# Order of the first products of the second block, and where the first tile's expert sums live, in a two-block transformer kernel on one core

## What is computed

```python
# first block, for each tile of 128 tokens
u = jnp.take(expert_u, eidx, axis=0)                      # 8 heads x 16 rows a token
h = jax.nn.gelu(jnp.einsum('thkd,td->thk', u, xb))
vv = jnp.take(expert_v, eidx, axis=0)
x = x + jnp.einsum('thk,thkd->td', (g * h), vv)
# second block
n = rmsnorm(x, norm_mix_pre);  proj = n @ w_in            # pool input, q, k, v, xq, gates
mem_n = rmsnorm(mem, norm_mem);  kv = mem_n @ w_mem_kv
# then stick-breaking attention, pooling, memory attention, gates, and a feed-forward
```

## Time and profile before

| what | value |
|---|---|
| three runs | 1216.73, 1220.64, 1221.88 us |
| profiled execution, its own time | 1221.03 us |
| its span in the trace | 1218.3 us, mean granted TensorE clock 0.981 |
| TensorE matmul busy | 1074.5 us (88%) |
| VectorE busy | 807.4 us (66%) |
| ScalarE busy | 387.3 us (32%) |
| GpSimd busy | 271.9 us (22%) |
| DMA | 372.42 MB, 306 GB/s over the span |

### The profile page before, as it was taken

The page is one execution under the profiler, slowest core; times in us unless marked ns, Lnnn a source line. Parts: engine busy times, 40 slices in busy tenths (PEclk is TensorE's granted clock), DMA queues, the critical chain, the costliest instruction groups (busy, mean ns, idle before and its releaser), DMA issues.

```text
span 1218.3 us, 12645 instructions
## 1 busy us (share of the span) xinstructions
PE 1074.5 (88%) x4502; PEld 701.4 (58%) x4502; DVE 807.4 (66%) x1681; ACT 387.3 (32%) x705; POOL 271.9 (22%) x261
## 2 busy tenths in 40 slices
PE   6988499889998886898877777789999999999997
PEld 5877355435543342444322222268877778999986
DVE  4666687877777677877787776554655476555543
ACT  5654221122112111310121011035765435444432
POOL 0000244454344343433433433300000000000000
PEclk8999799999999999899999999989999999999999
DMA  9734599999999999899999999985433434555440
GB/s 362 272 139 183 213 418 419 420 420 419 418 419 420 420 421 419 330 419 420 420 420 419 420 419 421 420 324 185 150 135 141 173 142 153 176 191 187 173 173 35
DMA packets 54381, 372.42 MB, mean 306 GB/s; under 512 B 6064, under 2 KB 7216, under 8 KB 10544
## 3 DMA queue, kind: packets, MB, share of 16 engines
q0 software_dynamic: 36864, 268.45, 53.2%
q1 hardware_dynamic: 17456, 103.17, 23.0%
HBM read 370.55 MB, written 1.05 MB: 305 GB/s over the span
## 4 chain that ended last, share of the span: by engine, by line
PE 59%; DMA 28%; DVE 8%; issue 3%; ACT 1%; POOL 1%; SPq 0%; DVEq 0%; POOLq 0%; ACTq 0%
DMA uv<-in_peer_uv,eidx 28%; PE bank L1787 15%; PE bank L1559 11%; PE bank L1560 11%; PE bank L1561 11%; PE bank L1622 5%; DVE uv L1301 3%; DMA wraw<-in_in1a 1%; DVE diag L1315 1%; DVE w_lo L1064 1%; PE bank L1531 1%; POOL uv L604 1%; ACT w_hi L676 1%; PE bank L1770 1%; PE bank L1720 1%
## 5 line engine op out<-in xcount | busy, mean ns | idle before, releaser
L1787 PE MATMUL bank<-uv,diag 128*128 128x512 f32 x1024 | 492.1, 610 | 102.8 <-DVE diag L1315 101.4
L1301 DVE SCALAR_TENSOR_TENSOR uv<-uv,xn 128x1024 f32<-128x1024 f32 x256 | 313.9, 1226 | 155.3 <-DMA uv<-in_peer_uv,eidx 153.3
L1787 PEld LDWEIGHTS bank<-uv,diag 128*128 128x128 f32 x1024 | 181.0, 191 | 377.7 <-issue 375.9
L604 POOL DMA_INDIRECT uv<-in_peer_uv,eidx x256 | 271.5, 1061 | 514.2 <-PE bank L1787 368.2
L1064 DVE TENSOR_TENSOR w_lo<-wraw,w_hi 128x2048 fp32r<-128x2048 f32 x76 | 173.7, 2291 | 138.1 <-ACT w_hi L676 138.1
L853 ACT ACTIVATE chosen<-chosen 128x1 f32<-128x1 f32 x256 | 51.9, 203 | 506.1 <-DVE uv L1301 506.0
L676 ACT CAST w_hi<-wraw 128x2048 fp32r<-128x2048 f32 x76 | 144.5, 1905 | 91.0 <-PE bank L1561 81.4
L1559 PE MATMUL bank<-nT_hi,w_hi 128*128 128x256 f32 x432 | 123.8, 287 | 3.2 <-DVE nT_lo L1076 3.2
L1560 PE MATMUL bank<-nT_lo,w_hi 128*128 128x256 f32 x432 | 123.4, 286 | 0.0
L1561 PE MATMUL bank<-nT_hi,w_lo 128*128 128x256 f32 x432 | 123.4, 286 | 0.0
L1315 DVE TENSOR_SCALAR diag<-const,chosen 128x128 f32<-128x128 f32 x256 | 88.3, 345 | 0.3 <-ACT chosen L853 0.3
(11 more groups left out here) (245 smaller groups left out, 1151.4 us busy)
## 6 DMA issues: line engine op xcount, KB each, us to landing
wraw<-in_ff_in SPq DMA_DIRECT2D x22, 1024.0 KB, 4.7
wraw<-in_ff_out SPq DMA_DIRECT2D x11, 1024.0 KB, 4.8
wraw<-in_query SPq DMA_DIRECT2D x4, 1024.0 KB, 8.9
uv<-in_peer_uv,eidx POOLq DMA_INDIRECT x256, 13.5
apart_last<-in_query SPq DMA_DIRECT2D x4, 512.0 KB, 11.0
wraw<-in_in_q SPq DMA_DIRECT2D x2, 1024.0 KB, 6.0
wraw<-in_in_k SPq DMA_DIRECT2D x2, 1024.0 KB, 10.1
wraw<-in_pool_o SPq DMA_DIRECT2D x2, 1024.0 KB, 4.7
```

What stands on the lines that cost most here:

```text
L604: pool.indirect_dma_start(out=uv[:, n % RING, :], out_offset=None, in_=io["peer_uv"], in_offset=bass.IndirectOffsetOnAxis(ap=eidx[:, head ...
L1301: nc.vector.scalar_tensor_tensor(out=u, in0=u, scalar=1.0, in1=xn[:, head // PEER_HEADS, :], op0=ALU.mult, op1=ALU.mult, accum_out=hdot[he ...
L1787: mm = nc.tensor.matmul(acc[m][:, :], diag[:, n % RING, :], uv[:, n % RING, D + m * HALF:D + (m + 1) * HALF], start=(n % (ROWS // NT) == 0 ...
```

## The change

1. In `psum_uses` tile 0's two sums stay in `held` until the memory's uses are given out; `memT` gets banks 4 to 7, `mk` 4, `mv` 5, and `nT` of tile 1 banks 2 and 3.
2. `in2_va` and `in2_vb` move from the front of the slots to the front of `q0`. `in2_va` is loaded among the rows, behind `mem_v`, and split into memory of its own (`w_hi_first`, `w_lo_first`): by ScalarE at head 14, k = 12, by VectorE at head 15, k = 2.
3. `in2_vb` is loaded behind the last row in four pieces of 512 columns and split by pieces (the wait on `row_free` is for row 251).
4. TensorE forms the values of tile 0 at once after the last row. Between the second and the third piece of `in2_vb` it turns tile 1. `keep_warm(14)` is gone. The root is taken from two half squares, and the normalisation is done in two halves.
5. In the last head `diagonal(n - 1)` stands ahead of `dot(n)`.
6. The slot loop has 15 slots; `XPT_SLOT` and `XO_SLOT` are two heads to a slot. `band` and `w_mix` are loaded behind `in2_pb`, after the values.

```diff
@@ psum_uses
     for j in [*range(EARLY, PEER_HEADS), *range(EARLY)]:
         use("query", j)
         use("route", j)
-    held.clear()
+    first = set(held)
     for n in range(2):
         held.add(use("expert", 1, n))
     both("memT")
     use("mk")
     use("mv")
+    held -= first
     both("nT")
+    for t in range(NT):
+        use("v2", t)
     held.clear()
@@
-XPT_SLOT, XO_SLOT = 12, 13
+XPT_SLOT, XO_SLOT = (12, 12, 13, 13), (13, 13, 14, 14)
@@ sync
-            load_blocks("mem_k", "mem_v")
+            load_blocks("mem_k", "in2_va")
 
             sp.wait_ge(row_loaded[(ROWS - 1) % RING], 16 * (ROWS // RING))
+            for q in range(KC // 2):
+                load_piece("in2_vb", q)
             load_blocks("in2_q0", "in2_k1")
             load_gain(4, "norm_mix_post_2")
+            load_blocks("in2_pa", "in2_pb")
+
+            wait_full(sp, "v2", NT - 1)
             sp.dma_start(band[:, :, :], io["band"]).then_inc(pool_loaded, 16)
             sp.dma_start(w_mix[:, :, :], io["w_mix"]).then_inc(pool_loaded, 16)
-            load_blocks("in2_va", "in2_g0a")
+            load_blocks("in2_x", "in2_g0a")
@@ scalar
+                elif head == LAST - 1 and k == 12:
+                    split_to("in2_va")
...
             load_table(ACT.Sqrt)
-            block_2_input(1)
-
-            split_to("in2_q0")
+            act.wait_ge(row_free, RING + ROWS - 4)
+            for q in range(2):
+                split_piece("in2_vb", q)
+            for m in range(2):
+                wait_read(act, "expert", 1, m)
+                half_square(x_sb[:, 1, half(m)], 3, 1, m)
+            for q in range(2, KC // 2):
+                split_piece("in2_vb", q)
             for h in range(2):
                 round_tile("nT", nT_hi, 1, h)
+            split_to("in2_q0")
+            copy_v(0)
             split_to("in2_q1")
+            copy_v(1)
             split_to("in2_k0")
-            split_to("in2_k1")
-            split_to("in2_va")
+            split_ahead("in2_q0")
+            split_ahead("in2_q1")
@@ vector
+                if head == LAST:
+                    diagonal(n - 1)
                 dot(n)
-                if n:
+                if n and head < LAST:
                     diagonal(n - 1)
...
+                if head == LAST and k == 2:
+                    split_to("in2_va")
             diagonal(ROWS - 1)
             add_experts(1)
-            norm(3, 1, x_sb[:, 1, :], xn[:, 1, :])
-            split_to("in2_q0")
+            dve.wait_ge(row_free, RING + ROWS - 4)
+            for q in range(2):
+                split_piece("in2_vb", q)
+            dve.wait_ge(gain_loaded[1], 16 * 2)
+            invert(3, 1)
+            for h in range(2):
+                nc.vector.scalar_tensor_tensor(out=xn[:, 1, half(h)], in0=x_sb[:, 1, half(h)], scalar=stat[:, 2, 7:8],
+                                               in1=gain[:, 1, half(h)], op0=ALU.mult,
+                                               op1=ALU.mult).then_inc(norm_ready if h else half_normed, 1)
+            for q in range(2, KC // 2):
+                split_piece("in2_vb", q)
             for h in range(2):
                 rest_tile("nT", nT_lo, nT_hi, 1, h)
-            split_to("in2_q1")
             split_to("in2_k0")
@@ tensor
-            keep_warm(14, "nT", 1, 0)
-            tile_T(3, "nT", xn, 1)
+            def turn_second():
+                for h in range(2):
+                    if h:
+                        pe.wait_ge(norm_ready, NT * 3 + 2)
+                    else:
+                        pe.wait_ge(half_normed, 1)
+                    transposes(xn[:, 1, half(h)], "nT", 1, h)
+            def values(p, t):
+                tokens_out(f"in2_v{p}", nT, lambda t: ("v2", t), turned="nT", tiles=(t,),
+                           between=turn_second if p == "b" else None)
+            for t in range(NT):
+                for p in "ab":
+                    values(p, t)
             for key in ("q2", "k2"):
                 for c in range(2):
-                    channels_out(f"in2_{key[0]}{c}", nT, key, c, turned="nT" if (key, c) == ("q2", 0) else None)
+                    channels_out(f"in2_{key[0]}{c}", nT, key, c)
```

More of the change, by code:

```diff
@@ L45 @@
 DEEP = 4
-SLOT_BLOCKS = (["in2_va", "in2_vb", "in2_pa", "in2_pb", "in2_x"]
+SLOT_BLOCKS = (["in2_pa", "in2_pb", "in2_x"]
                + [f"in2_g{n}{p}" for n in range(N_GATES) for p in "ab"])
@@ L52 @@
           + [f"out{n}{p}" for n in range(2) for p in "ab"] + ["mem"] + [f"query{j}" for j in range(PEER_HEADS)]
-          + ["mem_k", "mem_v", "in2_q0", "in2_q1", "in2_k0", "in2_k1"] + SLOT_BLOCKS
+          + ["mem_k", "mem_v", "in2_va", "in2_vb", "in2_q0", "in2_q1", "in2_k0", "in2_k1"] + SLOT_BLOCKS
           + ["x_o", "pool_o0", "pool_o1", "sb_o0", "sb_o1"] + [f"out2_{n}{p}" for n in range(2) for p in "ab"]
@@ L63 @@
 SPLIT_AT = {name: n for n, name in enumerate(SPLIT)}
+PIECED = ("in2_vb",)
+SPLIT_END, _parts = {}, 0
+for _name in SPLIT:
+    _parts += KC // 2 if _name in PIECED else 1
+    SPLIT_END[_name] = _parts
 RAW_USE = {f"query{j}": ("query", j) for j in range(PEER_HEADS)} | {"mem_k": ("mk",), "mem_v": ("mv",)}
@@ L116, in pair_at, with heads_at @@
     return p if (i - first) % 2 == 0 and 0 <= p < PAIRS else None
+def heads_at(i, slots):
+    return [h for h, slot in enumerate(slots) if slot == i]
 def psum_uses():
@@ L196, in psum_uses @@
             use("poolT", POOL_SLOT.index(i), among=one)
[L197 to L200, removed]
+        for h in heads_at(i, XO_SLOT)[::2]:
+            use("xoT", h // 2, among=z_banks)
+        for h in heads_at(i, XPT_SLOT):
+            use("xpT", h, among=z_banks)
         if name == "in2_x":
@@ L239, in rounded_order @@
             keys.append(("poolT", POOL_SLOT.index(i)))
-        if 0 <= i - XO_SLOT < XHEADS and (i - XO_SLOT) % 2 == 1:
-            keys.append(("xoT", (i - XO_SLOT) // 2))
+        for h in heads_at(i, XO_SLOT)[1::2]:
+            keys.append(("xoT", h // 2))
     keys += [("mergedT", t, h) for t in range(NT) for h in range(2)]
@@ L400, in two_block_kernel @@
         apart_loaded = [sem(f"apart_loaded{i}") for i in range(len(APART))]
+        piece_loaded = {name: [sem(f"piece_loaded_{name}{q}") for q in range(KC // 2)] for name in PIECED}
         w_rounded = sem("w_rounded")
@@ L473, in wait_loaded, with wait_piece @@
             b = BLOCK_AT[name]
-            eng.wait_ge(w_loaded[b % R_SLOTS], 16 * (b // R_SLOTS + 1))
+            eng.wait_ge(w_loaded[b % R_SLOTS], 16 * (b // R_SLOTS + 1 - sum(n in PIECED for n in IN_SLOTS[b % R_SLOTS:b:R_SLOTS])))
             return wraw[:, b % R_SLOTS, :]
+        def wait_piece(eng, name, q):
+            eng.wait_ge(piece_loaded[name][q], 16)
+            return wraw[:, BLOCK_AT[name] % R_SLOTS, half(q)]
         def wait_halves(eng, name):
@@ L488, in split_slot @@
                 return w_hi_last[:, :], w_lo_last[:, :]
+            if name == "in2_va":
+                return w_hi_first[:, :], w_lo_first[:, :]
             s = SPLIT_AT[name] % S_SLOTS
@@ L667, in split_to @@
                     s = split[0]
+                    assert SPLIT[s] not in PIECED
                     raw = wait_loaded(act, SPLIT[s])
-                    if s >= S_SLOTS and SPLIT[s] != "out1b":
+                    if s >= S_SLOTS and SPLIT[s] not in ("out1b", "in2_va"):
                         done = last_product(SPLIT[s - S_SLOTS])
@@ L676, in split_to, with split_piece @@
                     nc.scalar.copy(split_slot(SPLIT[s])[0], raw).then_inc(w_rounded, 1)
+                    split[0] += 1
+            def split_piece(name, q):
+                assert SPLIT[split[0]] == name
+                raw = wait_piece(act, name, q)
+                nc.scalar.copy(split_slot(name)[0][:, half(q)], raw).then_inc(w_rounded, 1)
+                if q == KC // 2 - 1:
                     split[0] += 1
@@ L1065, in split_to, with split_piece @@
                                             ALU.subtract).then_inc(w_split, 1)
+                    split[0] += 1
+            def split_piece(name, q):
+                assert SPLIT[split[0]] == name
+                dve.wait_ge(w_rounded, SPLIT_END[name] - KC // 2 + 1 + q)
+                hi, lo = split_slot(name)
+                nc.vector.tensor_tensor(lo[:, half(q)], wraw[:, BLOCK_AT[name] % R_SLOTS, half(q)],
+                                        hi[:, half(q)].bitcast(F32), ALU.subtract).then_inc(w_split, 1)
+                if q == KC // 2 - 1:
                     split[0] += 1
@@ L1431, in _ @@
                                           cols[:, 10 + 2 * c + a:11 + 2 * c + a]) for a in range(2)))
-                h = i - XO_SLOT
-                if 0 <= h < XHEADS and h % 2 == 1:
+                for h in heads_at(i, XO_SLOT)[1::2]:
                     c = h // 2
```

42 lines of the change are left out of this document (26 added, 16 removed).

## The result

| | before | after |
|---|---|---|
| runs | 6, median 1219.55 us (1216.63 to 1221.88) | 6, median 1206.30 us (1204.19 to 1208.30) |
| profiled execution, its own time | 1221.03 us | 1206.24 us |
| its span; mean granted clock | 1218.3 us; 0.981 | 1204.1 us; 0.986 |

The ratio is 0.990, with a 95% interval of [0.988, 0.992]: faster, by more than forecast. The span of the profiled execution fell by 14.2 us where the sum had 9.1.

The account below looks back on a forecast made before the run. DMA was taken to bound the rows, TensorE the stretch behind them and the slots. The terms -1.5 + 2.5 - 10.1 = -9.1 took 1221.0 to 1211.9 us, 1211.5 for the median; range 1207.5 to 1215.5.

Parts of the forecast that it names:

- Part 1, the banks: At the tiles' border, new banks for `memT` remove TensorE's 5.92 us wait: -1.5 us, bounds 0 and -5.0.
- Part 2, `in2_va`: Among the DMA-bound rows, loading this 1 MB block costs +2.5 us, bounds +2 and +3.5; its split costs 0.
- Part 3, the last row: Row 254 is done before, so only row 255's four instructions remain at the end: -1.5 us.
- Part 4: TensorE from the last row through k1 runs without long pauses at clock 1.00: -10.1 us with the last row's gain.
- The rule that spoke against the pieces: Loading `in2_vb`: some 2.0 us per transfer beside its bytes would make four pieces finish later than one block.
- One assumption in part 4: Behind the last row, TensorE without pauses over half a microsecond keeps clock 1.00, saving the slow clock's 2.7 us.
- Part 5, the slots: In the slot loop, moved loads and two slots fewer change nothing: 0, bounds 0 and +2 us.
- Idle DMA time in full at the border: Rival at the tiles' border: up to 5.0 us come back instead of 1.5, giving 1208 us; chance 0.12.
- The others: Remaining rivals: small waits around tile 1's turn 0.12, pieces paying singly 0.02, late `in2_vb` 0.02, border wait elsewhere 0.03.

Follow-up runs that it names:

- a_banks: The changed kernel with the memory's banks as before (`memT` on the banks of tile 0's sums): 1207.06 us, ratio 0.991.
- a_order: The changed kernel with `diagonal(n - 1)` behind `dot(n)` in the last head too, as before: 1206.91 us, ratio 0.992.
- b_again: The kernel before, unchanged, run once more for a second trace: 1216.37 us in its one run, span 1213.5 us.
- b_banks: The kernel before with the new banks alone (tile 0's sums held until the memory's banks are given out): 1217.71 us, ratio 0.9995.
- b_tile: The kernel before with only the `tokens_out` wait changed, to each turned tile's split instead of both tiles': 1216.22 us, ratio 0.998.
- b_pairs: The kernel before with only two heads of the memory attention to a slot, its 17 slots kept: 1215.66 us, ratio 0.998.
- a_apart: The changed kernel with the two heads' memory products in slot 13 apart, a head's transposes between them: 1206.35 us, ratio 0.990.
- a_halves: The changed kernel with squares, norm and turns by halves also at the norm ahead of the feed-forward: 1205.11 us, ratio 0.990.

## Why the prediction was off

**Part 1, the banks (-1.5).** Right in mechanism; the size is known only roughly. From row 136 on, after gains 0.9 us on the trace of before and 1.8 on a_banks. Set against before, the five traces with the old banks lose between 0 and 1.2 us from there on, 0.6 on the mean, and the eight with the new ones gain between 0.2 and 0.9, 0.7 on the mean: 1.3 us apart. Of the 5.0 us of idle DMA time that the mean share showed, that much could be won. This bears out the reading that most of the idle time of engines ahead of the others is no loss.

**Part 2, `in2_va` (+2.5).** +2.4 by row 128, as forecast. Its split made one dot 1.1 us late (row 243, 3.62 us behind its neighbour), and the next two made up for it, as forecast.

**Part 3, the last row (-1.5).** a_order gives -1.36 for it alone.

**Part 4 (with part 3, -10.1).** Measured -10.25 against the profiled execution. The first product comes 3.39 us after the last dot (3.8 was forecast), q0 at 15.8, k1's end at 39.0 (38.9 was forecast), the attention at 39.9. The halves of the square and of the norm and the removal of `keep_warm` were not undone one by one; that they hold nothing up is read from the timeline alone.

The rule that spoke against the pieces (the Trainium skill, page "DMA: Bandwidth & Descriptors", section "Anatomy of one DMA") is given there for transfers issued from GpSimd; these are SyncE's. As a cost that pieces in one queue pay one after another it doesn't hold here: the second piece was there within 3.8 us of the first issue, the whole block in one transfer at 4.85, and the four pieces win 1.6 us.

One assumption in part 4 was luck, and it hides in the agreement. The sum counted 2.7 us of slow clock in the row of before as a gain, and against that trace it is one. But b_again has the same pause and no fall, and b_banks and b_tile one of 1.5 us. The mean over the five traces of that order is 1.6 us, and none of the eight traces with the new order has a fall there. Against b_again, the same stretch gains 7.6 us and not 10.25.

**Part 5, the slots: "0, bounds 0 and +2". This step failed**, by -2.4. It looked for what pairing heads could delay, and never asked whether the paired products keep their price. Its bounds excluded a gain without a reason. The Trainium skill, page "TensorE: Matmul & The Clock Gate", section "Part 3: Packing small matmuls", has products of few columns with outputs on different partitions run side by side. b_pairs and a_apart agree, with 1.2 us a pair.

**A term that the sum left out: the wait per tile, -1.4.** The loop in `tokens_out` was read as what the new order of the values needs. It is a shared function, and the merge calls it as well. The wait that the edit takes away there was in the trace of before, 1.18 us at 991.74.

**The reference: -1.6.** The profiled execution held a fall of the clock at the merge that four other traces with the same wait don't have. So 1.6 us of the span's -14.2 are mostly that execution's own. (The change takes the wait away and with it the chance of such a fall, but at one trace in five that is an estimate of 0.3 us.)

**The account.** In spans: -9.1 forecast, -2.4, -1.4, -1.6, and +0.3 for the smaller differences, makes -14.2. The two things that the change does and the sum lacked would have put the forecast at 1207.7, just inside the range; the fall in the reference brings it below. Against b_again, which has neither of the falls behind the last row and at the merge, after is 9.4 us shorter (1213.5 to 1204.1). With the mean cost of these two falls, each over the five traces that have its wait (1.6 and 0.3), the change would be worth 11.3 us, an estimate. The medians of the result lie 13.2 us apart. The medians of the seven altered kernels of the second and third groups, each corrected by what its stretch costs or gains, lie 11 to 12 us below the kernel before on their chips, which is nearer to this estimate. How often the falls come was counted in these few traces, not in all runs.

**The rivals.** Idle DMA time in full at the border (1208) was nearest in time and wrong in cause: b_banks and a_banks show 0.9 to 1.8 us, not 5. The others did not come: TensorE waits neither at the turn nor for a piece of `in2_vb`, and its wait at the border is gone.

## What to carry to other kernels

Cost an edit in a shared helper at every call of it, and look in the trace for a wait that it removes there, before summing. When two small products are brought next to each other, ask whether they can run at once: a bound of "nothing to gain" needs a reason as much as one of "nothing to lose". And before a single profiled execution is taken as the reference, see which of its slow-clock stretches a second profile has too; here those alone were 4.2 us of 4.8 between two executions of one kernel.

## What was not expected of the hardware

- Two products with 64 columns of weights each, on different halves of the output partitions, in float32, take 1.09 us for eight instructions next to each other, and 1.08 us for four.
- The clock fell at the border in all five traces with TensorE's wait of some 6 us there, and in none of the eight without. Behind the pause of 2.1 us it fell in four of five, and behind the 1.2 us at the merge in one of five. In b_tile it fell at the start of the feed-forward, behind waits of 0.9, 0.6 and 1.05 us that twelve other traces have as well (a_halves a little shorter) without a fall. What a pause of 1 to 2 us costs is a chance and not a fixed value.
- At the border the new banks win 1.6 us by row 140, and after loses 0.7 of them again by row 176 (after's row 166 takes 3.48 us, before's 3.02). Perhaps the long wait had levelled the DMA engines, so that the rows behind it came without late ones; no run shows this.
